# Four regroupings around the merge: the SiLU of the convolution, a weight's low part, z's low parts, and two steps of projection D

## The reference, cut to what matters

```python
yc = silu(layer_norm(depthwise_conv(a * sigmoid(gate))))      # branch C, 512 channels
yd = sigmoid(o) * (mlstm_forward + mlstm_backward)            # branch D
for i in range(4):
    z += sigmoid(h @ w_gate[i] + b_gate[i]) * (y[i] @ w_branch[i])
out = z @ w_out
```

## Time and profile before

| | us |
|---|---|
| median of 3 runs (3562.60 to 3565.64) | 3564.94 |
| the profiled execution | 3567.71 |
| its span | 3565.90 |
| TensorE matmul busy | 3261.8 (91%) |
| VectorE busy | 2262.3 (63%) |
| ScalarE busy | 1732.9 (49%) |
| GpSimd busy | 704.8 (20%) |

### The profile page before, as it was taken

The page is one execution under the profiler, slowest core; times in us unless marked ns, Lnnn a source line. Parts: engine busy times, 40 slices in busy tenths (PEclk is TensorE's granted clock), DMA queues, the critical chain, the costliest instruction groups (busy, mean ns, idle before and its releaser), DMA issues. The chain is left out here.

```text
span 3565.9 us, 49308 instructions
## 1 busy us (share of the span) xinstructions
PE 3261.8 (91%) x18708; PEld 2750.8 (77%) x18708; DVE 2262.3 (63%) x3362; ACT 1732.9 (49%) x2169; POOL 704.8 (20%) x531
## 2 busy tenths in 40 slices
PE   7999889899999979999999399899899969999996
PEld 4987569799999757777777388578788757777885
DVE  3685871621222539999999584763313448999998
ACT  3112762422122547777776622754222347777775
POOL 3001012323322112222121100013344301111111
PEclk8999999999999979999999699999999979999998
DMA  7265025312221339999999244122233218999996
GB/s 262 79 168 141 5 77 181 93 50 101 84 92 50 137 116 336 334 330 334 337 334 349 76 101 102 33 97 76 86 112 95 96 72 310 350 343 352 362 359 249
DMA packets 445700, 647.09 MB, mean 181 GB/s; under 512 B 131662, under 2 KB 214078, under 8 KB 438622
## 3 DMA queue, kind: packets, MB, share of 16 engines
q1 hardware_dynamic: 304960, 557.88, 45.2%
q0 software_dynamic: 24096, 79.60, 6.8%
q10 hardware_dynamic: 116480, 7.35, 2.2%
HBM read 625.01 MB, written 27.08 MB: 183 GB/s over the span
## 5 line engine op out<-in xcount | busy, mean ns | idle before, releaser
L954 PE MATMUL ps<-hx,part 128*128 128x384 f32 (+2 forms) x5088 | 977.4, 352 | 16.7 <-POOL part L590 5.5
L954 PEld LDWEIGHTS ps<-hx,part 128*128 128x128 f32 x5088 | 883.5, 190 | 104.7 <-issue 16.9
L1416 PE MATMUL ps<-part,hx 128*128 128x512 f32 x3072 | 748.1, 396 | 19.8 <-DVE hx L2487 11.4
L1416 PEld LDWEIGHTS ps<-part,hx 128*128 128x128 f32 x3072 | 573.3, 189 | 152.4 <-issue 12.9
L2470 DVE TENSOR_TENSOR part<-raw,part 128x2048 fp32r<-128x2048 f32 x256 | 600.6, 2347 | 24.1 <-ACT part L1782 23.2
L1782 ACT ACTIVATE part<-raw 128x2048 fp32r<-128x2048 f32 x256 | 490.6, 1917 | 147.1 <-DMA raw<-in_w_exp_up 63.5
L590 POOL TENSOR_TENSOR part<-raw,part 128x2048 fp32r<-128x2048 f32 x66 | 303.8, 4603 | 638.6 <-ACT part L587 638.4
L1416 PE MATMUL ps<-hx 128*128 128x512 f32 x1536 | 379.6, 395 | 3.8 <-DVE hx L2470 1.3
L1416 PEld LDWEIGHTS ps<-hx 128*128 128x128 f32 x1536 | 286.7, 188 | 77.9 <-issue 7.7
L587 ACT ACTIVATE part<-raw 128x2048 fp32r<-128x2048 f32 x100 | 190.6, 1910 | 277.3 <-PE ps L954 159.9
L2470 DVE TENSOR_TENSOR hx<-raw,hx 128x2048 fp32r<-128x2048 f32 x128 | 294.2, 2298 | 31.0 <-ACT hx L1782 29.5
(11 more groups left out here) (314 smaller groups left out, 3679.6 us busy)
## 6 DMA issues: line engine op xcount, KB each, us to landing
raw<-in_w_exp_gate SPq DMA_DIRECT2D x128, 1024.0 KB, 6.0
raw<-in_w_exp_up SPq DMA_DIRECT2D x128, 1024.0 KB, 6.2
raw<-in_w_exp_down SPq DMA_DIRECT2D x128, 1024.0 KB, 6.6
raw<-in_w_mod SPq DMA_DIRECT2D x48, 1024.0 KB, 5.8
raw<-in_w_in SPq DMA_DIRECT2D x44, 1024.0 KB, 5.8
raw<-in_w_gate SPq DMA_DIRECT2D x32, 1024.0 KB, 5.3
raw<-in_w_branch SPq DMA_DIRECT2D x16, 1024.0 KB, 5.1
area<-rows_d POOLq DMA_DIRECT2D x40, 256.0 KB, 4.5
```

The source lines that it names most:

```text
L954: last = mm(dst, a, b, start=i == 0, stop=i == len(pairs) - 1)
L1416: last = mm(ps[:, bank, :], x, y, start=kh == 0 and a == 0, stop=kh == 1 and a == len(pairs) - 1)
```

## The change

It has four parts.

1. The SiLU of block j moves from the end of projection D into the merge, behind ScalarE's sigmoid of gate j of iteration 0. The signal `conv_normed` goes, since the stage barriers order the two.
2. The low part of the second O weight moves from GpSimd, at the end of the mLSTM, to VectorE, at the start of projection O. GpSimd waits there for it before its first load.
3. z's low parts of blocks 4, 5 and 6 move from behind the last sum to behind sums 1, 2 and 3 of the last iteration.
4. In projection D, `conv_sum` comes before group 5 and `turn_rows` before group 6 (they swap); on ScalarE `copy_rows` goes from copy 6 to copy 7 and `conv_root` from copy 14 to copy 13.

```diff
@@ GpSimd
-                split.mixers_to(l, S_O + 2)
                 st.leave()
 
+                split.mixers_from(l, S_O + 2)
                 load(ys[:, FB * TOK:2 * FB * TOK], yb_d).then_inc(*S("parked", l).by(16))
@@ TensorE
-                        {1: gate_sums, 2: turn_inputs, 3: turn_maxima, 5: turn_rows, 6: conv_sum, 12: conv_squares},
+                        {1: gate_sums, 2: turn_inputs, 3: turn_maxima, 5: conv_sum, 6: turn_rows, 12: conv_squares},
@@ ScalarE
                 def conv_silu(j):
-                    act.wait_ge(*S("conv_normed", l).at(j + 1))
                     fn(y_v[2][:, j, 0:nt], y_v[2][:, j, 0:nt], ACT.Silu, bias=conv_c[:, j, KS + 2:KS + 3],
...
-                       {4: gate_exps, 6: copy_rows, 7: lambda: (conv_square(0), conv_square(1)), 8: lambda: conv_square(2), 9: lambda: conv_square(3),
-                        14: conv_root})
-                for j in range(FB):
-                    conv_silu(j)
+                       {4: gate_exps, 7: lambda: (copy_rows(), conv_square(0), conv_square(1)), 8: lambda: conv_square(2),
+                        9: lambda: conv_square(3), 13: conv_root})
                 st.leave()
...
                         last.then_inc(*S("z_gate", l).by(1))
+                        if it == 0:
+                            conv_silu(j)
@@ VectorE
-                    V.tensor_tensor(y_v[2][:, j, 0:nt], y_v[2][:, j, 0:nt], cstd[:, 0:nt], ALU.mult
-                                    ).then_inc(*S("conv_normed", l).by(1))
+                    V.tensor_tensor(y_v[2][:, j, 0:nt], y_v[2][:, j, 0:nt], cstd[:, 0:nt], ALU.mult)
...
+                split.mixers_from(l, S_O + 1)
+                split.mixers_to(l, S_O + 2)
                 for g in range(2 * full):
...
                             if it == 2 * NBR - 1:
                                 z_low(j)
+                                if j:
+                                    z_low(FB + j - 1)
...
-                for k in range(FB, KD - 1):
-                    z_low(k)
                 st.leave()
```

More of the change, by code:

```diff
@@ L154 @@
 o_turned z_part z_sum z_hi z_lo ym_hi ym_lo p_y xn xn_hi h2_tmp xn_T left_in aff_out picked r_logits r_aff r_affT r_slotT g_out g_mm e_acc e_hid e_turned e_hH e_hL
-e_yH e_yL e_comb var std conv_sig conv_cent conv_var conv_std conv_normed m_abs m_log m_exps m_gate
+e_yH e_yL e_comb var std conv_sig conv_cent conv_var conv_std m_abs m_log m_exps m_gate
 p_var p_std z_gate r_cent r_exp e_sil q_mu q_std v_std v_nb xhat_n conv_part ab_part d_part ab_out d_out
```

## The result

| | before | after |
|---|---|---|
| median of 4 runs, us | 3565.29 | 3539.17 |
| the profiled execution's span | 3565.9 | 3535.7 |
| TensorE busy | 3261.8 | 3254.6 |
| ScalarE busy | 1732.9 | 1750.1 |
| VectorE busy | 2262.3 | 2270.5 |

The ratio, estimated over the runs, is 0.9922, 95% interval 0.9906 to 0.9937: 28 us faster (22 to 34). The medians differ by 26.1. 3538.3 was forecast.

What follows compares the result with a forecast made beforehand. TensorE bounds the kernel, and its idle times at the seams, with the lower clock after them, can be removed. Gains of 16.4 us (first layer) and 10.2 (second), together 26.6, from the median 3564.94 give 3538.3 us, range 3532 to 3547.

Steps and rivals of the forecast that it cites:

- Swap: Projection D: conv_sum fills TensorE's wait and group 5 runs at full clock; gain 4.2 us first layer, 0 second.
- `copy_rows` and the group-8 weight: Projection D: later copy_rows delays GpSimd's work on that weight, still hidden; 2 us to spare first layer, 0.4 to 0.8 second.
- SiLU out of D: End of projection D: without SiLUs the stage ends with its last copy; gain 5.1 us first layer, 4.2 second.
- Clock at the second mLSTM's start: Second layer's first mLSTM steps: transposes and outer products nearer full clock; gain 1.2 us (0 to 1.7).
- O weight: mLSTM's end: mask no longer slowed by GpSimd's subtraction; gain 5.0 us each layer, plus 0.7 in first layer's projection O.
- z's low parts: Merge's last iteration: low parts fill VectorE's waits for products; gain 1.4 us first layer, 0 second.
- SiLU in the merge: Merge's first iteration: added SiLUs and table loads on ScalarE; no loss first layer, 0.2 us second (0 to 1.5).
- a switch of 2.57: Rival, second merge: a switch costs twice the load, losing 6.7 us instead of 0.2; 3545 us, chance 0.06.
- a switch of 4.4 and more: Rival, merges: switches from 4.4 us eat the other gains, making the kernel slower; 3575 us at 5.1, chance 0.02.
- no gain at the O weight: Rival, mLSTM's end: mask and GpSimd meet by chance, the chain waits for something else; 10.7 us missing, 3549, chance 0.03.
- waits that go while the clock stays: Rival, TensorE's seams: less idleness but still granted 1.2 GHz; gain 20.8 us, so 3544, chance 0.10.
- a slow first group of projection O: Sign of being wrong: projection O's first matmuls still slow; 48 took 7.51 us before, 5.8 to 6.0 is full speed.

Runs made afterwards that it cites:

- a3: Kernel before with only TensorE's swap in projection D (conv_sum before group 5, turn_rows before group 6), ScalarE's steps unmoved; ratio to before 0.9986.
- a2: Kernel before with only the SiLU moved from the end of projection D into the merge; ratio to before 0.9964.
- c3: The changed kernel itself, unaltered, measured again on another occasion beside two other kernels; ratio to before 0.9929, median 3542.4 us.
- b1: Changed kernel with the second O weight's low part back on GpSimd, but at the start of projection O; ratio to before 0.9936.
- b2: Changed kernel with one tiny exponential behind each SiLU in the merge, adding a table load per gate; ratio to before 0.9942.
- a4: Kernel before with only z's low parts moved and ScalarE's copy_rows and conv_root moved, TensorE's order unchanged; ratio to before 0.9991.
- c4: Kernel before with 36 unread transposes ahead of the mLSTM's last products in both layers, the VectorE-GpSimd meeting left in; ratio to before 0.9986.
- a1: Kernel before with only the second O weight's low part moved to VectorE at projection O's start; ratio to before 0.9976.
- c1: b3 with GpSimd's load of the parked branch moved ahead of its wait for VectorE's low parts; ratio to before 0.9905, median 3535.1 us.
- b3: Changed kernel with two more low parts, of the merge's first weight and the first output weight, moved from GpSimd to VectorE; ratio to before 0.9906.
- b4: Changed kernel with unread matmuls at each merge's end and 12 unread transposes ahead of the second mLSTM's last products; ratio to before 0.9931.
- c2: c1 with b4's fillers and 8 more unread transposes behind the second layer's last mLSTM products; ratio to before 0.9908, median 3534.2 us.

## Why the prediction was right

The mechanism held: each part acted at the seam and by the wait that was named for it. Sizes were off, some up and some down.

- *Swap*, 4.2: 4.8 in the changed kernel and 4.8 in a3. It is above my upper end of 4.4, mostly since I gave `conv_sum` 1.4 us and group 5 starts 1.0 after it (567.31, 568.30). `copy_rows` and the group-8 weight: hidden in both layers, as worked out.
- *SiLU out of D*, 5.1 and 4.2: 5.1 and 4.2, in a2 alone as well.
- *Clock at the second mLSTM's start*, 1.2: 1.6 to 1.7, in a2 alone as well. It was at its upper end; in all nine traces with this part the first transposes took 0.66 us.
- *O weight*, first layer 5.0 + 0.7, second 5.0: the first trace gave 5.2 + 1.5 and 4.0. That this adds up to the 10.7 of the sum is luck. Means say it better. Four traces with the change or the same work in these stages (after, c3, b1, b2) have 95.2 and 74.6 us for mLSTM and O, three without O weight and SiLU (before, a3, a4) 101.8 and 80.7: 6.6 and 6.1. Of the second, 1.7 is the clock behind the SiLU, which leaves 4.4. So 6.6 where 5.7 stood and 4.4 where 5.0 stood. The wait was sized rightly, 3.8 in each layer; the clock's share is the term that was mis-sized, 2.8 and 0.6 where 1.9 and 1.2 stood. c4, which filled the idle time and left the meeting, found 2.1 and 0.7 for it, and one trace shows one draw of it. a1 and b1 show that the meeting with GpSimd was the cause. The Trainium skill (SBUF — State Buffer, section "Who interferes with whom") says that VectorE and GpSimd share a pair of SBUF ports as an exclusive lock, and that a VectorE instruction with two inputs in SBUF contends for it with a GpSimd instruction that reads SBUF. The traces agree: 4.50 us against 0.68, 3.49 against 0.42, 4.74 against 0.69, and the mask ended 0.5 us after GpSimd's subtraction.
- *z's low parts*, 1.4 and 0: 1.5 and 0.
- *SiLU in the merge*, a loss of 0.2: none. I counted both switches behind gate 1; but the sigmoid's table load began at 2531.80, about 0.8 us before that gate was ready (2562.02 before, less the 29.43 by which the runs differ there). The slack was 0.85 and 1.35, not 0.1, and b2 spent it: 4.4 us expected, 4.46 measured.
- *Not foreseen*: 1.6 us at the first merge's start, which comes and goes with the run (33.55 or 35.1 in kernels with the same code), and 2.3 us given back between the output projection and the second layer's mLSTM. That stretch, with 4.2 us added where the SiLU has left it, lasts 1306.4 to 1310.9 us over the kernels whose code is the same there. So neither can be put down to the change.

From group 4 to the second output projection the first trace is 27.3 us shorter than that of before: 28.0 by the terms of the sum (which had 26.6) and -0.7 by the two unforeseen ones. c3's trace of the same kernel is 24.8 shorter. So that the medians came out within 1 us of the forecast is partly luck; the gain is known to some 6 us.

Three of the rivals are refused: a switch of 2.57 (it was 1.30), a switch of 4.4 and more (b2), no gain at the O weight (a1). The first, waits that go while the clock stays, is refused where it had most to lose, at group 5 (8.78 us instead of 10.04) and at the second mLSTM's start (0.66 instead of 1.11), but it is partly right at the end of the mLSTM. One of my signs of being wrong was a slow first group of projection O. The first trace doesn't have it (6.00 and 6.03), c3 does in both layers (7.52 and 7.33), and the second layer's last products ran at clock 0.51 in the first trace. The ratio doesn't settle it: this rival's 20.8 us lie just outside the interval of the first measurement, 22 to 34, and inside that of c3, 20 to 31.

## What to carry to other kernels

Look for one engine's instruction whose duration in one place is several times its duration elsewhere (4.50 against 0.68 here), and see which engine works beside it; moving that work into a time when the slow one waits cost nothing here, with either engine (b1). Such a meeting mattered only where another engine waited for the slow instruction: the changed kernel still has 18 of them, and c1 gained by moving four. Before moving a wait, look at what stands behind it in its engine's queue: in the second layer's projection O b3 lost at a load what it had gained. Removing idle time ahead of matmuls can be worth more than that time, but the surplus isn't a fixed sum at a fixed place: compare stretches that hold all the idle times, over several traces.

## What the runs showed of the hardware

- The lower clock after short idle times moves between runs of the same code. With 2.25 us of idleness, 2 us of work and 1.87 us of idleness, the first layer showed 94.7 us in four traces and 96.4 in a fifth. The Trainium skill (TensorE: Matmul & The Clock Gate, section "What's actually happening") says that how many matmuls run slowly varies between runs of one kernel; c3 beside the first trace agrees (7.52 and 6.00 us).
- The longer idle time is followed by the lower clock more often. From the start of the last products to projection O it is 3.90 us at full clock. Behind 6.07 us of idleness it was 5.5 to 5.7 in all eight stretches (two layers of before, a2, a3 and a4), behind 2.25 us it was 4.8 to 5.4 in six of sixteen and 3.9 in the others. The first 48 matmuls of projection O then took 7.3 us or more in seven of the eight and in six of the sixteen.
- Filler matmuls brought the clock back at the end of the merges (2.08 to 1.20 us in the first layer, b4 and c2). For the two idle times of the mLSTM one trace each (73.84 us with one filled, 71.08 with both and the low part moved) can't part their effect from the scatter above.
- A table load for the switch between sigmoid and SiLU took 1.28 us sixteen times, and where its input was there the activation began 1.29 to 1.30 us after the load did. The figure of the Trainium skill (ScalarE: Activation LUTs, section "What ACT_TABLE_LOAD costs"), 2.66 us with a drain, isn't borne out. By an estimate from that figure and the prediction's sum for a dear switch, 7 x 2.66 - 11.3, the second merge would have lost 7.3 us, and it lost none.
